# The queries' rotation of the last attention: one fp32 product replaced by two fp32r products of a high and a low part

## The reference, cut to what matters

```python
def rotary(x, pos):
    ...
    x1, x2 = xf[..., :half], xf[..., half:]
    return jnp.concatenate([x1 * cos - x2 * sin, x2 * cos + x1 * sin], axis=-1).astype(x.dtype)

        ...
            q = rotary((hn @ swa_w_q[j]).reshape(B, S, SWA_Q_HEADS, HEAD_DIM), pos)
            o = sliding_window_sink_attention(q, k_shared, v_shared, swa_sinks[j])
            h = h + o.reshape(B, S, SWA_Q_HEADS * HEAD_DIM) @ swa_w_o[j]
```

## Time and profile before

| | |
|---|---|
| median of 3 runs | 2180.22 us (2179.17 to 2180.49) |
| the profiled execution | 2181.89 us, of which the span of its instructions is 2180.1 us |
| TensorE, busy share of the span | 98% (ScalarE 60%, VectorE 73%, GpSimd 27%) |
| mean granted TensorE clock | 0.996 |
| the stage `swa` with its output projection | about 1910.5 to 1982.5 us of the span |

### The profile page before, as it was taken

One profiled execution on the slowest core, in us unless ns is written; L12 is line 12 of the kernel. 1 busy time (PEld: TensorE's weight loads), 2 busy tenths in 40 slices (PEclk: granted clock), 3 DMA queues, 4 the chain that ended last, 5 costly groups with the idle time before them and its releaser, 6 DMA issues.

```text
span 2180.1 us, 39606 instructions
## 1 busy us (share of the span) xinstructions
PE 2134.7 (98%) x14203; PEld 1924.9 (88%) x14203; DVE 1600.1 (73%) x1903; ACT 1300.5 (60%) x1801; POOL 584.6 (27%) x450
## 2 busy tenths in 40 slices
PE   8999899999999999999999999999999999999998
PEld 7889889888888999999888888999888888888887
DVE  7876888886887677666887687645887688677874
ACT  5664776664665565665665566454665466456663
POOL 3431662440342000000342243000442144122430
PEclk9999999999999999999999999999999999999999
DMA  6665467665566555454566466544566566534662
GB/s 208 192 197 178 127 199 247 193 207 188 164 192 216 167 165 164 153 158 142 172 192 210 158 192 218 166 140 142 166 192 210 162 192 200 187 105 145 192 219 99
DMA packets 371157, 387.92 MB, mean 178 GB/s; under 512 B 11334, under 2 KB 366031, under 8 KB 371056
## 3 DMA queue, kind: packets, MB, share of 16 engines
q1 hardware_dynamic: 357104, 369.14, 53.7%
q10 hardware_dynamic: 13952, 17.41, 2.5%
HBM read 376.02 MB, written 10.49 MB: 177 GB/s over the span
## 4 chain that ended last, share of the span: by engine, by line
PE 88%; DVE 7%; ACT 3%; issue 1%; POOL 0%; DMA 0%; ACTq 0%; DVEq 0%
PE ps L822 43%; PE ps L823 23%; PE ps L776 3%; PE ps L777 3%; PE ps L778 3%; DVE wlo L1691 1%; DVE xg L1709 1%; PE ps L797 1%; PE ps L866 1%; PE ps L798 1%; PE ps L799 1%; PE ps L868 1%; PE ps L867 1%; ACT whi L1282 1%; PE ps L1007 1%
## 5 line engine op out<-in xcount | busy, mean ns | idle before, releaser
L822 PE MATMUL ps<-xg,whi 128*128 128x512 f32 x2816 | 981.7, 391 | 5.3 <-DVE wlo L1691 1.9
L1691 DVE TENSOR_TENSOR wlo<-raw,whi 128x1024 fp32r<-128x1024 f32 (+2 forms) x652 | 881.6, 1363 | 139.3 <-ACT whi L1282 138.4
L1282 ACT ACTIVATE whi<-raw 128x1024 fp32r<-128x1024 f32 (+2 forms) x652 | 720.5, 1113 | 190.6 <-PE ps L823 130.4
L823 PE MATMUL ps<-xg,wlo 128*128 128x256 f32 x2816 | 794.6, 282 | 0.0
L822 PEld LDWEIGHTS ps<-xg,whi 128*128 128x128 f32 x2816 | 529.4, 188 | 119.1 <-DVE xg L1709 3.5
L823 PEld LDWEIGHTS ps<-xg,wlo 128*128 128x128 f32 x2816 | 533.0, 189 | 0.2
L822 PE MATMUL ps<-hT,whi 128*128 128x512 f32 x1408 | 488.5, 390 | 0.0
L823 PE MATMUL ps<-hT,wlo 128*128 128x256 f32 x1408 | 397.1, 282 | 0.0
L822 PEld LDWEIGHTS ps<-hT,whi 128*128 128x128 f32 x1408 | 264.4, 188 | 55.4
L2193 POOL TENSOR_TENSOR gate_r<-gate,r 128x512 f32<-128x512 f32 x88 | 189.7, 2155 | 287.8 <-DVE gate L1769 287.8
L823 PEld LDWEIGHTS ps<-hT,wlo 128*128 128x128 f32 x1408 | 266.1, 189 | 0.0
(11 more groups left out here) (276 smaller groups left out, 2993.1 us busy)
## 6 DMA issues: line engine op xcount, KB each, us to landing
raw<-in_ffn_w_in SPq DMA_DIRECT2D x352, 512.0 KB, 3.5
raw<-in_ffn_w_out SPq DMA_DIRECT2D x64, 768.0 KB, 4.7
raw<-in_ffn_w_out SPq DMA_DIRECT2D x64, 640.0 KB, 4.7
raw<-in_w_kv SPq DMA_DIRECT2D x48, 512.0 KB, 3.5
raw<-in_a_w_in SPq DMA_DIRECT2D x32, 512.0 KB, 4.5
raw<-in_b_w_q SPq DMA_DIRECT2D x24, 512.0 KB, 3.8
raw<-in_sb_w_qkv SPq DMA_DIRECT2D x24, 512.0 KB, 4.2
bias_by_distance<-bias_rows ACTq DMA_DIRECT2D x12, 768.0 KB, 5.4
```

Source lines behind the costliest of these rows:

```text
L822: nc.tensor.matmul(out, whi[:, par, w], both, start=first and k == 0, stop=False)
L823: mm = nc.tensor.matmul(out[:, 0:T], wlo[:, par, w], both[:, 0:T], start=False, stop=last and k == total - 1)
L1282: nc.scalar.activation(whi[:, par, off:off + size], raw[:, 2 * par + half, :size], ACT.Copy).then_inc(hi_done, 1)
L1691: nc.vector.tensor_tensor(wlo[:, par, off:off + size], raw[:, 2 * par + half, :size], whi[:, par, off:off + size].bitcast(F32), ALU.subtra ...
```

## The change

The rotation of each unit becomes two fp32r products, of a high and a low part of `sw_t`. ScalarE copies the constant `rot` once into an fp32r tile, `sw_turner` (the two formats of the permutation's 0, 1 and -1 are the same number). For each unit ScalarE rounds `sw_t` to `sw_thi` and VectorE subtracts to get `sw_tlo`; both tiles have one buffer. TensorE waits for the two parts separately.

On ScalarE the rounding stands between the two halves of `whi`, so that the second half of tick t is rounded behind `sw_thi` of unit t. On VectorE the subtraction stands directly behind `sw_t`, ahead of `late(t)`; it waits for ScalarE.

```diff
 region = ExitStack()
     sw_t = sb("sw_t", [P, 2, 2 * T], F32, region)
+    sw_thi = sb("sw_thi", [P, 2 * T], F32R, region)
+    sw_tlo = sb("sw_tlo", [P, 2 * T], F32R, region)
+    sw_turner = sb("sw_turner", [P, P], F32R, region)
...
+    sw_thid, sw_tlod, sw_const = sem("sw_thid"), sem("sw_tlod"), sem("sw_const")
...
(TensorE, swa, early)
-                    nc.tensor.matmul(ps[:, SW_OUT, :], const("rot"), sw_t[:, u % 2, :], start=True, stop=True).then_inc(sw_rot, 1)
+                    pe.wait_ge(sw_const, 1)
+                    pe.wait_ge(sw_thid, u + 1)
+                    nc.tensor.matmul(ps[:, SW_OUT, :], sw_turner[:, :], sw_thi[:, :], start=True, stop=False)
+                    pe.wait_ge(sw_tlod, u + 1)
+                    nc.tensor.matmul(ps[:, SW_OUT, :], sw_turner[:, :], sw_tlo[:, :], start=False, stop=True).then_inc(sw_rot, 1)
...
(ScalarE, swa)
                     if t == 0:
                         split_high(*ahead_of(st, 0, 0), (0,))
                         stage_norm("swa")
-                    split_high(*ahead_of(st, t // 2, t % 2), (0, 1) if t else (1,))
+                        nc.scalar.activation(sw_turner[:, :], const("rot"), ACT.Copy).then_inc(sw_const, 1)
+                    split_high(*ahead_of(st, t // 2, t % 2), (0,) if t else ())
+                    act.wait_ge(evac_done, st["fill"] + t + 3)
+                    if t:
+                        act.wait_ge(sw_rot, t)
+                    nc.scalar.activation(sw_thi[:, :], sw_t[:, t % 2, :], ACT.Copy).then_inc(sw_thid, 1)
+                    split_high(*ahead_of(st, t // 2, t % 2), (1,))
...
(VectorE, swa)
                     scaled(sw_t[:, t % 2, :], st["fill"] + t, e, HD ** -0.5)
+                    dve.wait_ge(sw_thid, t + 1)
+                    nc.vector.tensor_tensor(sw_tlo[:, :], sw_t[:, t % 2, :], sw_thi[:, :].bitcast(F32), ALU.subtract).then_inc(sw_tlod, 1)
                 late(t)
```

## The result

The changed kernel is slower by more than forecast: 2189.45 us, the median of 5 runs (2188.34 to 2194.55), against 2180.48 before (2179.17 to 2180.95). The ratio is 1.0041, with a 95% interval of 1.0029 to 1.0053. Forecast were 2185.2 and at most 2187.2. The same kernel run again beside 23 runs of the one before gave 2188.31 against 2181.05, a ratio of 1.0030 (1.0016 to 1.0045).

What follows compares the result with a forecast made beforehand. In `swa` the prediction took VectorE and ScalarE as the path, TensorE beside it, though TensorE bound tick 0. 1.17 + 0.99 + 2.11 + 0.68 = +4.95 us, giving a median of 2185.2 us (+0.23%), range 2182.6 to 2187.2.

Steps and rivals of the forecast that it cites:

- tick 0: First tick of `swa`: TensorE's normal products resume later, behind the blocked `sw_tlo`(0) and the low product, +1.17 us.
- tick 1: Second tick of `swa`: masks(0) start later behind `sw_tlo`(1), +0.99 us, sum so far +2.16.
- tick 2: Third tick of `swa`: masks(1) start later behind `sw_tlo`(2), +2.11 us, sum +4.27.
- tick 3: Fourth tick of `swa`: `sw_thi`(3) between the two `whi` on ScalarE delays `sw_oT`(0), +0.68 us, sum +4.95.
- GpSimd blocks the subtraction: `sw_tlo` on VectorE waits for GpSimd's `sw_c` and ends 0.55 us behind it; the sum is 4.95, without it 3.3.
- TensorE's saving is hidden: In `swa`, the shorter rotation saves TensorE 0.40 us a unit, 1.6 in all, only if TensorE were the bound.
- The rival without blocking: `sw_tlo` on VectorE starts when its input is there: sum 3.3 us, 2183.5 (+0.15%), chance 0.20.
- the one in which all is hidden: `sw_thi` and `sw_tlo` fill idle time of ScalarE and VectorE, TensorE's 1.6 us shows: 2178.6, chance 0.08.
- TensorE's clock falls on top: New idle time on TensorE in `swa` lowers its clock, 1.7 us on top of 4.95: 2186.9, chance 0.10.
- The list of new waits: TensorE's added idle: about 1.6 us before scores(1), 2 before the transposes, 1 before the values, 1 before `out_slot`(0).
- It is 1.67 above the median: Whole kernel: profiled execution 2181.89 lies 1.67 us over the median 2180.22, so 2186.8 becomes a median of 2185.2.
- not slower: Whole kernel: outcome of no change by the 0.2% (4.4 us) line, 0.38, or faster, 0.02; slower had 0.60.

Runs made afterwards that it cites:

- after_again: The changed kernel run again unchanged, for a second profile and timed runs beside the kernel before: stage 63.50 us, ratio 1.0030.
- cos_later: Changed kernel, but GpSimd's product with the cosine also waits for VectorE's subtraction of the same unit: stage 62.18 us, ratio 1.0024.
- low_on_gpsimd: Changed kernel, but unit 0 keeps the full fp32 product and units 1 to 3 have the subtraction on GpSimd: stage 59.06 us, ratio 1.0001.
- high_only: Changed kernel without `sw_tlo` and the low product, so only the high fp32r product rotates: stage 59.54 us, ratio 1.0006.
- low_behind: Changed kernel with VectorE's subtraction moved behind `late(t)`, so after `sw_oT` and the masks: stage 61.78 us, ratio 1.0016.
- after: The changed kernel's first profile, nothing else altered: profiled execution 2188.42 us, stage 64.98 us.
- after_c: The changed kernel unchanged, run for another profile: stage 65.62 us.
- after_d: The changed kernel unchanged, run for one more profile: stage 65.00 us.
- first_only: Changed kernel with only unit 0 split; units 1 to 3 keep the full fp32 product: stage 61.33 us, ratio 1.0013.

## Why the prediction was wrong

**What held: every term of the sum.** In the profile where the clock stayed up (after_again), counted from the start of `sw_t`(0):

| step | before | after_again | moved by | forecast |
|---|---|---|---|---|
| `sw_t`(1), end of tick 0's cost | 4.71 | 6.00 | 1.29 | 1.17 |
| `sw_nmax`(0), tick 1 | 9.06 | 11.33 | 2.27 | 2.16 |
| `sw_nmax`(1), tick 2 | 18.03 | 22.41 | 4.38 | 4.27 |
| `sw_oT`(0), tick 3 | 25.77 | 30.84 | 5.07 | 4.95 |
| last `sw_oT` | 58.50 | 63.50 | 5.00 | 4.95 |

The 0.1 that it is off comes in tick 0, behind a TensorE that had stood still: the low product has 0.51 there and 0.39 in the second rotation, where it follows the high product at once. GpSimd blocks the subtraction (cos_later), TensorE's saving is hidden (low_on_gpsimd, high_only), TensorE waits 2.03 for the masks before L1175 ("some 2 us"), and nothing behind the stage gives back or takes more (201.5 to 201.6 in every profile). The rival without blocking is wrong, since `sw_tlo` takes 1.20 and 1.41 and not 0.69; the one in which all is hidden is wrong by its time, as the stage is 5 us longer.

**The first step that failed: "TensorE's clock falls on top", with 0.10.** Its mechanism and nearly its price were right: 1.5 where it said 1.7. But it is the usual case and not an unlikely rival. The clock fell in the stage in three of the changed kernel's four profiles, and in four of the six that have its waits around the first rotation. I set it low by one row, the 4.32 of 6.8 us busy that went by at 1.00, and missed where the new idle time would be worst. The list of new waits named four places, in ticks 2 to 4; the place where the clock fell first in each case was the first rotation. The working of tick 0 held the numbers for it: `sw_thi` delays TensorE's first product from 1920.76 to 1921.4, and the low one waits for 1922.6, so nearly all of 1919.9 to 1922.6 is idle. They were used for the delay and not for the clock. With 5.0 + 1.5 the profile's 6.5 comes out.

**The second: "It is 1.67 above the median".** The clock alone doesn't take the result out of the range: 1.5 more on 2185.2 is 2186.7, under the upper end of 2187.2. The sum was worked out on a profiled execution of 2181.89 and then set down by 1.67 to the median of three runs, 2180.22, which lay within 1.3 us. Those three were short ones. Over all 79 runs of the kernel before that were made with these experiments, the times go from 2179.16 to 2187.55 and the median is 2181.78, so that the profiled execution was an ordinary one. Without the 1.67, 2181.89 + 5.0 + 1.5 gives 2188.4: the profiled execution of the changed kernel took 2188.42, and its seven later runs have a median of 2188.31. The range had 0.9 for all such spread, where the first part alone, the same program, spreads over 6.6 us.

**What is left of 9.0.** The four stages have a mean of 64.78 and the two of before one of 58.54: 6.2, or 0.29% of the time, just at the lower end of the first interval and inside the second. The other 2.8 us of the first comparison lie outside the stage as far as profiles show. Half of them, 1.3, is that the first five runs of before (2180.48) lie under the 2181.78 of all. The 14 runs of the changed kernel have a mean of 2189.83, the 79 of before one of 2182.34, which are 7.5 apart. Why this is 1.3 more than the stage's 6.2, no run here tells; that it was chance in `hgrn` is argued, not shown.

**The other side.** The ending "not slower" was given 0.38 + 0.02, and "slower" 0.60 by a margin of 0.6 us over the 0.2% line. The clock's 1.5 and not a better knowledge of the sum put the result clearly over it, so that "slower" came true partly by luck.

## What to carry to other kernels

Cheaper products were worth nothing in this stage, where TensorE waits; the operations that prepare the operands were the price, and their place in the other engines' order decided it: 5.0 ahead of the masks, 3.3 behind them, and for units 1 to 3 alone 3.7 ahead of the masks and 0.6 on the engine that was free. Before VectorE gets another instruction with two SBUF inputs, look at what GpSimd does at that moment. And when a change makes TensorE wait, add up its idle time place by place, new and old together, and look whether the clock holds there; here it cost 1.5 on top of the 1.3 of tick 0, in some executions only. Before a forecast of a few us starts from a median of three runs, look at how far a larger number of runs spreads.

## What the runs showed of the hardware

The same idle times of TensorE (1.56 and 0.68 around one product) left the granted clock at 1.00 in two executions (after_again, low_behind) and were followed by some 3.4 us at the lower level in four (after, after_c, after_d, first_only), where the products of 256 columns start 0.21 us apart in place of 0.12. One profile of a kernel therefore doesn't settle whether a wait costs clock.

A blocked VectorE instruction was recorded as long as its wait plus its work: `sw_tlo` 1.21 to 1.40 for 0.69, `wlo` 2.27 for 1.22. Its end stood 0.54 behind the end of GpSimd's instruction for 512 elements. The lists of waits don't show it, because the time counts as busy.

The same eight VectorE multiplications beside GpSimd's work took 3.6, 4.6 or 6.2 us in different executions of the same instructions, and the length of the first 1920 us goes with it.
